# Masking the second head's first group ahead of the gate's take, in the first period of a gated delta net layer

## The reference

```python
proj = h @ w_in
qkv = silu(causal_dwconv(qkv, conv_w))
q = l2norm(q.reshape(bsz, L, GDN_HEADS, GDN_DK)) * (GDN_DK ** -0.5)
k = l2norm(k.reshape(bsz, L, GDN_HEADS, GDN_DK))
...
kk = einsum('bhcid,bhcjd->bhcij', kc, kc)
tri = where(strict, bc[..., :, None] * kk * decay, 0.0) + eye(CHUNK)
sol = triangular_solve(tri, rhs, lower=True, unit_diagonal=True)
...
def step(S, inp):                       # over the chunks of a head
    v_new = u_c - einsum('bhid,bhde->bhie', w_c, S)
    o = einsum('bhid,bhde->bhie', qd_c, S) + einsum('bhij,bhje->bhie', qk_c, v_new)
    S = cd_c[..., None, None] * S + einsum('bhid,bhie->bhde', kd_c, v_new)
```

## Time and profile before

| | us |
|---|---|
| median of 3 runs | 1307.53 |
| lowest and highest | 1307.06, 1307.54 |
| the profiled execution, time | 1307.65 |
| the profiled execution, span | 1305.9 |

### The profile page before, as it was taken

The page is one execution under the profiler, slowest core; times in us unless marked ns, Lnnn a source line. Parts: engine busy times, 40 slices in busy tenths (PEclk is TensorE's granted clock), DMA queues, the critical chain, the costliest instruction groups (busy, mean ns, idle before and its releaser), DMA issues.

```text
span 1305.9 us, 24372 instructions
## 1 busy us (share of the span) xinstructions
PE 1283.7 (98%) x9309; PEld 1085.8 (83%) x9309; DVE 957.8 (73%) x1543; ACT 690.4 (53%) x1100; POOL 16.5 (1%) x16
## 2 busy tenths in 40 slices
PE   6999999999999999999999999999999999999998
PEld 4788888888888998989887777788888989999876
DVE  7778778875767878777767777885777777776655
ACT  6766676765563434344446777733634444343452
POOL 0000000000000000000001000000000000000100
PEclk9999999999999999999999999999999999999999
DMA  4332222322234342333232222133243332322232
GB/s 162 79 92 63 77 77 69 81 66 82 72 107 132 96 125 91 105 96 98 65 98 81 65 65 71 59 97 113 83 159 97 98 96 96 98 96 88 75 95 97
DMA packets 40733, 119.52 MB, mean 92 GB/s; under 512 B 3984, under 2 KB 11600, under 8 KB 40656
## 3 DMA queue, kind: packets, MB, share of 16 engines
q1 hardware_dynamic: 33184, 114.78, 28.5%
q10 hardware_dynamic: 7472, 3.70, 1.7%
HBM read 116.34 MB, written 2.13 MB: 91 GB/s over the span
## 4 chain that ended last, share of the span: by engine, by line
PE 94%; DVE 3%; DMA 1%; ACT 1%; issue 1%; SPq 0%; ACTq 0%; DVEq 0%
PE acc L429 13%; PE acc L431 12%; PE acc L430 12%; PE ps L873 6%; PE ps L871 6%; PE ps L872 6%; PE acc L855 4%; PE acc L856 4%; PE acc L854 4%; PE ps L856 4%; PE ps L855 4%; PE ps L854 4%; PE ps L977 1%; PE ps L962 1%; PE ps L989 1%; DMA work<-rows 1%
## 5 line engine op out<-in xcount | busy, mean ns | idle before, releaser
L429 PE MATMUL acc<-xh,wh 128*128 128x512 f32 x624 | 259.2, 415 | 9.7 <-DVE xl L2598 8.8
L431 PE MATMUL acc<-xh,wl 128*128 128x512 f32 x624 | 244.6, 392 | 0.0
L430 PE MATMUL acc<-xl,wh 128*128 128x512 f32 x624 | 244.6, 392 | 0.0
L405 DVE TENSOR_TENSOR wl<-raw,wh 128x1024 fp32r<-128x1024 f32 x111 | 135.8, 1225 | 55.9 <-ACT wh L398 54.0
L429 PEld LDWEIGHTS acc<-xh,wh 128*128 128x128 f32 x624 | 117.9, 189 | 35.6 <-DVE wl L405 9.8
L431 PEld LDWEIGHTS acc<-xh,wl 128*128 128x128 f32 x624 | 117.6, 188 | 26.0
L430 PEld LDWEIGHTS acc<-xl,wh 128*128 128x128 f32 x624 | 118.0, 189 | 20.9 <-issue 1.2
L398 ACT ACTIVATE wh<-raw 128x1024 fp32r<-128x1024 f32 x111 | 115.8, 1049 | 29.7 <-DMA raw<-in_weights 20.3
L1495 ACT ACTIVATE wh<-raw 128x1024 fp32r<-128x1024 f32 x48 | 50.9, 1061 | 111.0 <-PE ps L856 111.0
L856 PE MATMUL acc<-yh,wl 128*128 128x512 f32 x256 | 99.9, 390 | 0.0
L855 PE MATMUL acc<-yl,wh 128*128 128x512 f32 x256 | 99.8, 390 | 0.0
(11 more groups left out here) (356 smaller groups left out, 2900.7 us busy)
## 6 DMA issues: line engine op xcount, KB each, us to landing
raw<-in_weights SPq DMA_DIRECT2D x208, 512.0 KB, 3.6
work<-rows ACTq DMA_DIRECT2D x14, 256.0 KB, 6.9
h<-in_xT SPq DMA_DIRECT2D x4, 512.0 KB, 6.6
outT<-h SPq DMA_DIRECT2D x8, 256.0 KB, 2.4
cst<-in_cst SPq DMA_DIRECT2D x1, 512.0 KB, 4.8
work<-in_pT SPq DMA_DIRECT2D x1, 512.0 KB, 4.6
kept<-in_keep SPq DMA_DIRECT2D x1, 208.0 KB, 6.2
work<-in_w_ab SPq DMA_DIRECT2D x1, 128.0 KB, 7.4
```

Of the source, the lines that this page charges most:

```text
L405: nc.vector.tensor_tensor(lo[:], raw[u.const % 2][:], hi[:].bitcast(F32), ALU.subtract).then_inc(lo_done, 1)
L429: nc.tensor.matmul(dst[:], hi, mh[:, k, :], start=(n == 0), stop=False)
L430: nc.tensor.matmul(dst[:], hi, ml[:, k, :], start=False, stop=False)
L431: mm = nc.tensor.matmul(dst[:], lo, mh[:, k, :], start=False, stop=(n == KT - 1))
```

## The change

In period 1 the call `dve_masks(dve, 1, 0, True, True)`, which masks both results of x(0), goes from behind `scales()` to directly behind v's taps. It now stands in front of the gate's take, the split of unit 6, q's mask and the two scales. In the later periods the call stays where it was, moved into the branch `if i > 1`.

```diff
@@ -2034,6 +2034,7 @@
                 dve_ti(dve, 1)
                 for _ in dve_taps(dve, 2, 0):
                     pass
+                dve_masks(dve, 1, 0, True, True)
                 dve_gate(dve, 0)
                 split_lo(dve, Unit(first))
                 dve_qkd(dve, 0)
@@ -2044,8 +2045,8 @@
             ahead = i + 1 < H
             if b > 0:
                 dve_osum(dve, b)
-            dve_masks(dve, i, 0, True, early)
             if i > 1:
+                dve_masks(dve, i, 0, True, early)
                 dve_gate(dve, b)
             dve_updates(dve, i, 0, True, early)
             if b > 0:
```

## The result

The changed kernel is slower. Its median is 1310.1 us (20 runs, 1308.21 to 1310.94) against 1307.64 us for the kernel before (20 runs, 1307.04 to 1309.55). The ratio is 1.0015, with a 95% interval of 1.0008 to 1.0022: 1.0 to 2.9 us slower, and 2.46 us between the medians. The profiled execution took 1309.31 us with a span of 1307.5.

The account below looks back on a forecast made before the run. PE's work bounds the kernel, so only its waits can pay: 1.88 us gained at tx(0), 1.88 given back at tx(2), 0.1 from sooner rows, forecast 1307.4 us. Own range 1307.0 to 1307.8, wider range 1306.4 to 1308.3.

Parts of the forecast that it names:

- What bounds the kernel, and the chain: PE, busy 1283.7 of 1305.9 us; tx(2) waits on v's taps, rows, ACT's decay and tap, DVE's taps and mask.
- (a): At tx(0): masks end before PE's last weight matmul, so its wait goes; local gain 1.88 us.
- (b): The three DVE jobs the masks pass start 0.28 us later, cost 0; the late update comes 0.91 us earlier.
- (c): x(1) to x(2) run 1.88 us earlier; unit 7's split only 1.23, still leaving cover of 0.28 us.
- (d): At tx(2): its start stays at 73.20, the wait grows from 0.97 to 2.85 us, the 1.88 gain is given back.
- (e): Head 2's rows on ACT's DMA queue: SP's load starts 0.28 us later, so they land 0.1 us sooner.
- the two bounds of 0.99 and 0.9: Ends for the rows' landing term: a gain of 0.99 us, a loss of 0.9 us.
- the slower one with the clock: Behind tx(2)'s longer wait PE's clock falls; nine matmuls cost 1.8 us more, time 1309.2; chance 0.05.
- The size against no change: Measurement tells about 0.2%, 2.6 us, from no change; same had 0.95, faster 0.02, slower 0.03.

Follow-up runs that it names:

- e5: The change, with head 2's row DMAs issued by ACT ahead of the silu of v; median 1305.77 us against 1307.51 for the kernel before, ratio 0.9988.
- e1: The change as it is, run and profiled again against the kernel before; median 1309.97 us against 1307.91, ratio 1.0015.
- e17: The kernel before, unchanged, run again for its fifth profile; span 1309.8 us.
- e4: The change, with SP's loads from unit 8 on held back until the rows landed; median 1308.58 us, ratio 1.0004 to the kernel before.
- e18: The changed kernel as it is, run again for its fifth profile; span 1309.7 us.
- e12: The kernel before, unchanged, run once more for its profile; span 1306.0 us.
- e9: e5 plus one unused DVE multiplication between head 2's k taps and the mask of tx(2); median 1307.59 us.
- e8: The change with rows issued early and two more steps of unit work in front of tx(2); median 1304.27 us, ratio 0.9974 to the kernel before.
- e7: The change, with two more steps of unit work moved between x(2) and tx(2); median 1307.76 us, ratio 0.9998 to the kernel before.
- e10: e5 plus three unused DVE multiplications between head 2's k taps and the mask of tx(2); median 1309.87 us.
- e11: e10 plus six added matmuls in front of tx(2) whose product is thrown away; median 1308.17 us.

## Why the prediction was wrong

- **What bounds the kernel, and the chain: right.** tx(2) hangs on the rows, through ACT's decay and tap and DVE's taps. e5 took the rows out and L636 starts at 71.19, against 74.11 in e1.
- **(a) Right.** tx(0) no longer waits; L1910 starts at 58.12.
- **(b) Right.** The three jobs start later (the gate's take at 58.39, not 58.26) and nobody waits for them. The late update follows the scales at 60.86, against 61.01 in the working. L429 behind x(1) has no wait.
- **(c) Right.** Unit 7's split starts at 64.20, released by L398; L588 does not wait.
- **(d) Right in its mechanism, short in its sum.** The wait in front of L636 was to be 2.85 us and is 3.26 to 4.29 in five profiles. The whole gain went there. In the first profile, 3.40, PE was through at 70.14 instead of 70.35 and L636 started at 73.54 instead of 73.20. But the step stopped at tx(2), and the text behind the sum says that behind 74 us everything runs as before. That sentence is the step that failed: it put the clock behind the longer wait at nothing. From L636 to L681 the change takes 5.04 us in the mean of five profiles, the kernel before 3.61 (with e17) or 3.13 (the other four): 1.4 to 1.9 us. The difference of the mean spans, 1308.2 to 1306.8, is 1.4. Up to L515, which takes in the low clock behind L681, the median of the five is 5.86 us against 3.79: 2.07 of the 2.46 us between the medians of the result. The other 0.4 us are not resolved; L636 starts 0.15 us later in the mean of the five, and whether the change has a part in that stays open.
- **(e) Wrong.** I took the fall from 172 to 97 packets a us for the work of the load. In e4 the rate falls to 92 with no load beside it. And in the kernel before the load has no packet until 65 us, though it was issued at 60.25, while the rows fall from 157 packets in 63 to 64 us to 102 in 64 to 65. It is this stretch, and not 60 to 61 us, that shows the two queues not taking turns. The rows took 8.86 us where the term had them sooner than 8.39. They vary by 1.5 us between executions of the kernel before, so the two bounds of 0.99 and 0.9 were nearer the mark than the 0.1 that I took.
- **The rival that came true** was the slower one with the clock. It had the right place, the right sign and nearly the right price: 9 x 0.2 = 1.8 us against 1.46 to 2.43 (4.58 to 5.55, less 3.12), or up to 2.9 where the clock is still low at L681 (e18: 6.67 us to L515, less 3.79). It was given 0.05 and lay outside the range. Two readings led there. I took the 0.23 us behind the 1.88 us wait as a property of a wait of that length; e12 shows the low clock behind 1.89 us in the same program, and nine of 11 executions of e9, at about 2.0, have a lower mean clock and a time to match. One profile showed one outcome of a chance. And I took 2.85 as "nearer" to 1.88 than to 8.76 and let that stand for a small chance, where nothing in the rows said so.
- **Not seen at all**: the wait in front of tx(2) can have a use. In e12 it hid most of a low clock that began behind tx(0). How often it does is not shown. The change moved the whole wait to the last place of the period, where no wait of this period comes behind it.
- **The size against no change.** The centre of the result, 0.15% slower, lies within the 0.2% that I called no change. The price of the clock was known to stay within it. The range was still too narrow, since 1308.3 left out a case that needed only one row to be read otherwise.

## What to carry to other kernels

When a change removes one wait of PE and a later one grows by the same, don't book a zero: a merged wait is longer, and matmuls behind it may run at the lower clock with nothing left to absorb them. Ask of each wait what it hides from the waits ahead of it. And look for what ends the last one: issuing two transfers 6.7 us earlier and moving two steps of work into the gap made the same reordering 3.2 us faster than the kernel before.

## What the hardware showed that I had not expected

- The lower clock comes by chance at these lengths. With no wait in the period (e8) the 8 executions lie within 0.6 us. At 1.43 us (e5) most of 11 lie near 1305.5 and four above 1306.3. At 1.89 us (e7) seven of 11, at 2.02 us (e9) nine of 11 are in the slower group with the lower mean clock, at 3.46 us (e10) all are 1308.66 or more. The profiles of the change, 3.26 to 4.29 us, are low in all five. Once low, it costs 1.4 to 2.9 us here (L636 to L515 takes 5.24 us in e9 and 6.73 in e17, against 3.79 at the full clock); the higher figures come where L636 itself already runs at it (1.06 instead of 0.64 us).
- It need not begin directly behind the wait: in e12 five weight matmuls, in e11 three, run at full pace first.
- Two transfers of 256 KB each from DRAM in small packets took 8.2 to 9.8 us to the later landing, in two programs whose DMAs are the same, on different executions. Without the load beside them it was 8.92, in one profile.
